# Recurrent layers of a two-block transformer kernel: the gate projection moved behind the head products, the latents behind the query projection, GpSimd made to wait

## What is computed

```python
proj = h @ w_in[l]
c_q, c_kv, k_pe, hq, hf, hi, hg = jnp.split(proj, splits, axis=-1)
a = _mla(c_q, c_kv, k_pe, positions, q_a_norm[l], w_q_b[l], kv_a_norm[l], w_kv_b[l])
r = _hgrn2(hq, hf, hi, hg, lower[l], hg_out_norm[l]).astype(x.dtype)
x = x + jnp.concatenate([a, r], axis=-1) @ w_out[l]
# in _mla: c_q and c_kv are normalized and go through w_q_b and w_kv_b, the rotary parts are
# rotated, then causal scores, softmax, and the product with v
# in _hgrn2: f from hf, q = silu(hq), v = hi, and at the end
o = _rmsnorm(o, out_norm) * jax.nn.silu(g_raw)      # g_raw is hg
```

## Time and profile before

| | us |
|---|---|
| median of 3 runs | 1895.46 |
| lowest, highest | 1894.84, 1895.87 |
| time of the profiled execution | 1896.17 |
| its span in the profile | 1893.6 |
| TensorE busy | 1864.6 |
| VectorE busy | 1530.8 |
| ScalarE busy | 1239.9 |
| GpSimd busy | 404.6 |

### The profile page before, as it was taken

One profiled execution on the slowest core, in us unless ns is written; L12 is line 12 of the kernel. 1 busy time (PEld: TensorE's weight loads), 2 busy tenths in 40 slices (PEclk: granted clock), 3 DMA queues, 4 the chain that ended last, 5 costly groups with the idle time before them and its releaser, 6 DMA issues.

```text
span 1893.6 us, 26114 instructions
## 1 busy us (share of the span) xinstructions
PE 1864.6 (98%) x9344; PEld 1566.7 (83%) x9344; DVE 1530.8 (81%) x1654; ACT 1239.9 (65%) x1484; POOL 404.6 (21%) x206
## 2 busy tenths in 40 slices
PE   9999999999999999999999999999999999999997
PEld 6888889888878888877888888888888888888886
DVE  6745357777776887697699999999999999999997
ACT  6654444444744444464488888888888888888876
POOL 6856870002724000372540000000000000000100
PEclk9999999999999999999999999999999999999999
DMA  9534556665443676444599999999999999999994
GB/s 286 169 120 134 178 182 229 227 219 180 139 139 118 214 239 224 158 125 138 181 386 396 391 383 376 384 397 369 389 365 389 396 363 388 367 389 396 367 396 185
DMA packets 251540, 524.19 MB, mean 277 GB/s; under 512 B 9960, under 2 KB 58736, under 8 KB 251328
## 3 DMA queue, kind: packets, MB, share of 16 engines
q1 hardware_dynamic: 243408, 504.00, 74.4%
q10 hardware_dynamic: 5824, 12.06, 1.7%
q0 software_dynamic: 2224, 7.01, 1.2%
HBM read 507.71 MB, written 15.34 MB: 276 GB/s over the span
## 4 chain that ended last, share of the span: by engine, by line
PE 88%; DVE 6%; ACT 2%; DMA 1%; issue 1%; POOL 1%; SPq 0%; DVEq 0%; ACTq 0%
PE bank L736 24%; PE bank L738 24%; PE bank L737 24%; PE bank L1097 6%; PE bank L1100 3%; DMA arena<-in_w_in 1%; PE bank L1363 1%; PE bank L859 1%; PE bank L832 1%; DVE arena L2440 1%; POOL w_lo_sb L665 1%; DVE arena L1944 1%; DVE arena L2431 1%; PE bank L838 0%; DVE arena L2454 0%
## 5 line engine op out<-in xcount | busy, mean ns | idle before, releaser
L1989 DVE TENSOR_TENSOR w_lo_sb<-arena,w_hi_sb 128x1024 fp32r<-128x1024 f32 x672 | 807.8, 1223 | 73.8 <-ACT w_hi_sb L1517 43.7
L1517 ACT ACTIVATE w_hi_sb<-arena 128x1024 fp32r<-128x1024 f32 x672 | 711.3, 1062 | 168.5 <-PE bank L738 167.8
L736 PE MATMUL bank<-w_hi_sb,left_sb 128*128 128x512 f32 (+1 forms) x1400 | 553.1, 395 | 2.1 <-POOL w_lo_sb L665 2.0
L738 PE MATMUL bank<-w_hi_sb,left_sb 128*128 128x512 f32 (+1 forms) x1400 | 542.2, 387 | 0.0
L737 PE MATMUL bank<-w_lo_sb,left_sb 128*128 128x512 f32 (+1 forms) x1400 | 541.5, 387 | 0.0
L1537 ACT ACTIVATE w_hi_sb<-arena 128x1024 fp32r<-128x1024 f32 (+1 forms) x269 | 278.4, 1052 | 301.4 <-PE bank L738 218.7
L665 POOL TENSOR_TENSOR w_lo_sb<-arena,w_hi_sb 128x1024 fp32r<-128x1024 f32 (+1 forms) x134 | 342.6, 2576 | 546.3 <-ACT w_hi_sb L1537 545.7
L736 PEld LDWEIGHTS bank<-w_hi_sb,left_sb 128*128 128x128 f32 x1400 | 263.1, 188 | 58.8 <-POOL w_lo_sb L665 5.3
L738 PEld LDWEIGHTS bank<-w_hi_sb,left_sb 128*128 128x128 f32 x1400 | 262.9, 188 | 54.8
L737 PEld LDWEIGHTS bank<-w_lo_sb,left_sb 128*128 128x128 f32 x1400 | 263.4, 188 | 50.7 <-issue 0.7
L736 PE MATMUL bank<-w_hi_sb,hid_hi_sb 128*128 128x512 f32 x656 | 257.3, 392 | 0.1
...
...
## 6 DMA issues: line engine op xcount, KB each, us to landing
...
```

The costliest lines, as they stand in the source:

```text
L736: pe.matmul(out, still[0], moving[0], start=start, stop=False)
L738: return pe.matmul(out, still[1], moving[0], start=False, stop=stop)
L1517: act.activation(expert_buffer(w_hi_sb, j), expert_piece(j % MOE_SUBS), ACT.Copy) \
L1989: dve.tensor_tensor(expert_buffer(w_lo_sb, j), expert_piece(j % MOE_SUBS), expert_buffer(w_hi_sb, j).bitcast(F32), ALU.subtract) \
```

## The change

In `gemm_plan` the output gate `hg` moves from behind `hq` to behind the last head product, so that the latents `c0` and `c1` and the values `hi` come three or four pieces earlier. The order on each engine follows. On TensorE the turned decay matrices stand between the pieces of `c0` where they stood between those of `hg`, level 0 follows in `c1`, level 1 and the turned latents in `hi`; the later levels are spread anew, and level 5, the turned rotary parts, both scores, level 6 and level 7 go between the four pieces of `hg`. On ScalarE the pieces of `hg` are made between the exponentials of levels 4, 5 and 6, and the gate is read with a Silu behind the softmax. On VectorE `normalize_c` stands ahead of two levels more; the maxima are taken as minima of negated scores, so that the negations go, for tile 1 in two halves; the gate's multiplication with its gain moves from the middle to the place in front of `gate_hgrn`. GpSimd waits for level 7 ahead of the first piece of `wo`.

```diff
         w = f"w_in_2_{layer}"
         add(f"hf_{layer}", w, base + 512, 512)
         add(f"hq_{layer}", w, base, 512)
-        add(f"hg_{layer}", w, base + 1536, 512)
         add(f"c0_{layer}", w, 0, 512)
         add(f"c1_{layer}", w, 512, base - 512)
...
             add(f"kvb{i}_{layer}", f"w_kv_b_2_{layer}", 512 * i, 512, KV_RANK // P)
+        add(f"hg_{layer}", w, base + 1536, 512)
         add(f"wo_{layer}", f"w_out_2_{layer}", 0, D)
         if layer == 0:
...
-                 (f"hqT_{layer}", 2), *level[0:4], (f"cT_{layer}", 3), *level[4:6], (f"hst_{layer}", 1),
-                 (f"mpT_{layer}", 3), level[6], (f"msc0_{layer}", 2),
-                 level[7], (f"msc1_{layer}", 2), (f"ho_{layer}", 2), (f"mP_{layer}", 3), (f"mo_{layer}", 2),
+                 (f"hqT_{layer}", 2), *level[0:2], (f"cT_{layer}", 3), *level[2:5], (f"hst_{layer}", 1), level[5],
+                 (f"mpT_{layer}", 3), (f"msc0_{layer}", 2), level[6],
+                 (f"msc1_{layer}", 2), level[7], (f"ho_{layer}", 2), (f"mP_{layer}", 3), (f"mo_{layer}", 2),
...
+                        if j == span[f"hg_{l}"][1]:
+                            pool.wait_ge(sem(f"level_ready_{l}"), len(LEVELS))
                     pool.wait_ge(sem("w_hi_ready"), hi_count[j])
                     pool.tensor_tensor(buffer(w_lo_sb, j, k, n), w, buffer(w_hi_sb, j, k, n).bitcast(F32),
...
-                gemm(f"hg_{l}", between={1: turn_gate, 3: turn_queries})
-                gemm(f"c0_{l}", between={0: lambda: level(0), 3: lambda: level(1)})
-                gemm(f"c1_{l}", between={1: lambda: level(2)})
-                gemm(f"hi_{l}", between={0: lambda: level(3), 2: turn_c})
+                gemm(f"c0_{l}", between={1: turn_gate, 3: turn_queries})
+                gemm(f"c1_{l}", between={0: lambda: level(0)})
+                gemm(f"hi_{l}", between={1: lambda: level(1), 3: turn_c})
+                level(2)
                 pe.wait_ge(sem("pair_read"), pair_end[f"cT_{l}"])
...
-                        level(4)
+                        level(3)
                 for i in range(2):
...
+                        level(4)
                 pe.wait_ge(sem("n_kt_ready"), l + 1)
                 b = pair(f"hst_{l}", 0)
...
-                level(6)
-                pe.wait_ge(sem("pair_read"), pair_end[f"mpT_{l}"])
...
-                    if t == 1:
-                        level(7)
+                def turn_rotated():
+                    level(5)
+                    pe.wait_ge(sem(f"m_rot_{l}"), 2 * T)
...
+                def scores(t):
+                    if t == 0:
+                        pe.wait_ge(sem("pair_read"), pair_end[f"mpT_{l}"])
+                        pe.wait_ge(sem("gemm_read"), gemm_at[f"kvb1_{l}"] + T)
...
+                    level(6 + t)
+
+                gemm(f"hg_{l}", between={0: turn_rotated, 1: lambda: scores(0), 2: lambda: scores(1)})
...
-                split_to(span[f"hg_{l}"][0] + 2)
+                split_to(span[f"c0_{l}"][0] + 2)
...
-                split_to(span[f"c0_{l}"][0] + 2)
+                split_to(span[f"c0_{l}"][1] + 2)
...
                 evacuate(f"hq_{l}", by_token(n_q, 0, func=ACT.Silu))
-                evacuate(f"hg_{l}", by_token(n_g, 0, func=ACT.Silu))
...
                 level_exp(2)
-                evacuate(f"c0_{l}", by_token(n_c, 0))
-                level_exp(3)
...
-                level_exp(4)
+                level_exp(3)
                 evacuate(f"hi_{l}", by_token(n_v, 0))
                 evacuate_heads(f"qb0_{l}", n_mqT[:, 0:2, :], n_pq[:, :, 0:128])
-                level_exp(5)
+                level_exp(4)
                 evacuate_heads(f"qb1_{l}", n_mqT[:, 2:4, :], n_pq[:, :, 128:256])
                 evacuate_heads(f"kvb0_{l}", n_mkT[:, 0:2, :], n_vm[:, :, 0:256])
+                split_to(span[f"hg_{l}"][0] + 2)
+                level_exp(5)
+                evacuate_heads(f"kvb1_{l}", n_mkT[:, 2:4, :], n_vm[:, :, 256:512])
+                split_to(span[f"hg_{l}"][1])
                 level_exp(6)
-                evacuate_heads(f"kvb1_{l}", n_mkT[:, 2:4, :], n_vm[:, :, 256:512])
                 level_exp(7)
-                split_to(span[f"kvb1_{l}"][1] + BUFFERS)
-                softmax(n_sc, MLA_HEADS, row_max, f"m_max_ready_{l}", f"m_exp_{l}", keys=(P, TOKENS))
-
+                for t in range(T):
+                    split_to(span[f"hg_{l}"][1] + 1 + 2 * t)
+                    for i in range(MLA_HEADS):
+                        act.wait_ge(sem(f"m_max_ready_{l}"), 1 if t == 0 else 2 + i // 2)
+                        part, at = n_sc[:, t, i, 0:(t + 1) * P], t * MLA_HEADS + i
+                        act.activation(part, part, ACT.Exp, bias=row_max[:, at:at + 1], scale=-1.0,
+                                       accum_out=row_sum[:, at:at + 1]).then_inc(sem(f"m_exp_{l}"), 1)
...
                 level_scale(2)
+                normalize_c()
                 level_take(1)
-                level_diff(4)
-                level_scale(3)
-                level_take(2)
-                normalize_c()
-                rotate(lambda t: n_c[:, t, Q_RANK + KV_RANK:].rearrange("p (h d) -> p h d", h=1), 1)
-                level_take(3)
                 for i in range(3):
                     n = min(2, 5 - 2 * i)
                     b = tiles(bank_of(f"cT_{l}", i)[:, 0:n * TOKENS], n)
                     mul(n_cT[:, 2 * i:2 * i + n, :], b, over(c_gain[l][:, 2 * i:2 * i + n], 2, TOKENS), "pair_read")
+                rotate(lambda t: n_c[:, t, Q_RANK + KV_RANK:].rearrange("p (h d) -> p h d", h=1), 1)
+                level_diff(4)
+                level_scale(3)
+                level_take(2)
+                level_diff(5)
                 level_scale(4)
-                level_diff(5)
-                gains = n_g[:, :, :].rearrange("p t (g d) -> p (t g) d", d=P)
-                mul(gains, gains, over(hg_gain[l], 1, 8))
-                level_take(4)
-                level_scale(5)
+                level_take(3)
                 level_diff(6)
                 dve.wait_ge(sem("gemm_read"), gemm_at[f"qb1_{l}"] + T)
                 rotate(lambda t: n_pq[:, t, :].rearrange("p (h d) -> p h d", h=MLA_HEADS), MLA_HEADS)
+                level_scale(5)
+                level_take(4)
+                level_diff(7)
+                copy_out(f"hst_{l}", 0, n_st)
                 level_scale(6)
                 level_take(5)
-                level_diff(7)
-                copy_out(f"hst_{l}", 0, n_st)
                 for i in range(2):
                     copy_out(f"mpT_{l}", i, n_pqT[:, 2 * i:2 * i + 2, :].rearrange("p k c -> p (k c)"), ROPE)
                 copy_out(f"mpT_{l}", 2, n_pkT, ROPE, TOKENS)
                 level_scale(7)
-                level_take(6)
...
-                    masked_scores(f"msc{t}_{l}", n_sc, MLA_HEADS, (NOPE + ROPE) ** -0.5, causal, [t], (P, TOKENS))
-                    part = row_max[:, t * MLA_HEADS:(t + 1) * MLA_HEADS]
-                    link(dve.tensor_reduce(part, n_sc[:, t, :, 0:(t + 1) * P], AX_X, ALU.max))
...
-                    negate(part, part, f"m_max_ready_{l}")
...
+                    for i in range(2):
+                        heads = slice(2 * i, 2 * i + 2)
+                        b = tiles(bank_of(f"msc{t}_{l}", i)[:, :])
+                        dve.scalar_tensor_tensor(n_sc[:, t, heads, keys], b[:, :, keys], -(NOPE + ROPE) ** -0.5,
+                                                 over(causal[:, t, keys], 1, 2), ALU.mult, ALU.subtract) \
+                            .then_inc(sem("pair_read"), 1)
+                        dve.wait_ge(sem("pair_read"), told("pair_read"))
+                        if (i + 1) * 2 % each == 0:
+                            lo, hi = (i + 1) * 2 - each, (i + 1) * 2
+                            dve.tensor_reduce(row_max[:, t * MLA_HEADS + lo:t * MLA_HEADS + hi], n_sc[:, t, lo:hi, keys],
+                                              AX_X, ALU.min).then_inc(sem(f"m_max_ready_{l}"), 1)
+                    level_take(6 + t)
...
-                split_out(f"mixT_{l}", banks=range(0, 2), freed=span[f"hi_{l}"][1])
+                split_out(f"mixT_{l}", banks=range(0, 2), freed=span[f"hg_{l}"][1])
+                dve.wait_ge(sem("gemm_read"), gemm_at[f"hg_{l}"] + T)
+                gains = n_g[:, :, :].rearrange("p t (g d) -> p (t g) d", d=P)
+                mul(gains, gains, over(hg_gain[l], 1, 8))
                 gate_hgrn()
```

28 lines of the change are left out of this document (13 added, 15 removed).

## The result

| | before | changed |
|---|---|---|
| median of the runs, us | 1895.15 | 1913.41 |
| lowest to highest of four | 1894.23 to 1895.87 | 1910.13 to 1913.85 |
| profiled execution, us | 1896.17 | 1910.13 |
| its span, us | 1893.6 | 1907.8 |
| mean granted clock in it | 0.999 | 0.993 |

The ratio is 1.0092, with an interval of 1.0078 to 1.0107: slower by 18 us. I had forecast slower by 8.6 (1904), with a range to 1908. The direction holds, the size does not.

The account below looks back on a forecast made before the run. TensorE, busy 1864.6 of 1893.6 us, was taken to bound the kernel. Part A -1.6, part B 0 and part C +10.2 gave +8.6 us on 1895.46: 1904.1, rounded to 1904, with a range from 1889 to 1908.

Parts of the forecast that it names:

- Part A: From the first piece of c1 (500.27 in layer 0) to the head products: +0.2 us in layer 0, -1.8 in layer 1.
- part B: From head products to output projection: 4.4 us of old waits filled, 4.4 of new ones made, 0 in each layer.
- part C: Behind the output projection's start: gate products late behind GpSimd's pieces, TensorE waits 5.1 us in each layer.
- the near tie at 4.3: In part C, GpSimd arrives at 4.26, just before VectorE's first reciprocal product ends at 4.30; otherwise the wait is 2.7 us.
- Costs nothing: Extra table load and gate read on ScalarE, SyncE's load queue, and GpSimd's wait for level 7: all hidden, 0 us.
- Rivals 1 to 3: Late gate product costs little, 1894.5 to 1896.3, chance 10; near tie VectorE's way, 1899.3, 12; part B opens, 1895.3, 10.
- Rival 4: Projection pieces fill TensorE's holes and VectorE never waits for GpSimd: -9.8 us, 1885.7, chance 10.
- Rival 5: The clock falls too behind the 5.1 us wait of part C: 4.4 us in all, 1908.5, chance 8.

Follow-up runs that it names:

- e9: The changed kernel with the copy of the state bank ahead of level 7's two subtractions on VectorE: 1914.83 us.
- e10: The changed kernel with level 6's scale on VectorE moved behind the three copies of the turned rotary parts: 1903.22 us.
- e8: The changed kernel without its holding of GpSimd for level 7 before the first piece of the output projection: 1913.27 us.
- e2: The changed kernel with 14 unread matmuls on TensorE before it waits for the gate products: 1910.42 us.
- e1: The changed kernel, GpSimd also waiting before the output projection's fifth piece until VectorE has made both gate products: 1899.42 us.
- e7: The kernel of e1 with 8 unread matmuls on TensorE just ahead of the scores of tile 0: 1894.85 us.
- e5: e1 with state-bank copy, level 5's take and rotary copies ahead of level 7's subtractions and level 6's scale; turned queries given own memory: 1886.95 us.

## Where the prediction was right and where it failed

**The waits were right.** Part A was forecast at +0.2 and -1.8, and came to -0.3 and -2.0. VectorE's chain in part B came out nearly as written: waits of 1.56 and 2.29 for 2.0 and 2.4, the copies at 550.5 against the 29.5 us behind the head products that I had counted (it was 29.2). e9 and e10 show that the two reasons given for them hold, one by one. In part C, VectorE met GpSimd three times, in the order written down, and the products were ready 12.76 us behind the output projection instead of 13.4: 4.5 us a layer for 5.1. The part's own uncertainty, the near tie at 4.3, did go GpSimd's way: its piece began at 4.22, and the second multiplication by the reciprocal waited for it. "Costs nothing" held for the holding at level 7 (e8).

Without the clock, the terms sum to -0.8 (ahead of A), -2.3 (A), +1.3 (B, from 52.33 and 52.30 against 51.68 and 51.64) and +9.0 (C): +7.2, where I had +8.6. That they come so close is in part luck: B came out 1.3 higher, and A, the stretch ahead of it and C 2.7 lower in all. One small sum was off: the work between 550.86 and 574.08 comes to 17.1 us by the figures given with it, not 17.3, so 6.1 us were lost there and not 5.9. No term of the forecast hangs on it.

**The clock was the failing step.** The sum had no term for it. It stood among the rivals, for part C alone, with a chance of 8 and a price of 4.4. What the runs show in its place: behind the waits of part C it costs 3.0 (e2) to 3.7 us (the table), at most 5.0 (all of e1's 14.0 that isn't its waits of 9.0). That is close to the price, but it happens in both layers of every profile that has these waits, so its chance should have been the forecast's. Behind part B's waits it costs 4.6 (e7 against e1), and that was not in the text at all, though I had forecast both waits, 2.0 and 2.4, with one piece of 2.7 us between them. Together that is 7.6 to 9.6 us, about half of the 18.3 that were lost. The experiments price only the one and a half dips that part B of e1 has. The profile of e8, which has all four, gives the whole by the marks of the table: 3.1 and 3.2 us behind part B's waits (55.47 twice, against 52.33 and 52.30) and 2.8 and 1.6 behind part C's (14.61 and 13.38 from `turn_mix` to the next bank, against 11.78 and 11.79), 10.7 in all. With the 7.2 above that is 17.9, and its span is 18.0 longer than that of the kernel before (1911.6 against 1893.6). So nothing else of size is missing from the sum.

I went wrong in how I read the earlier trace rows: the clock fell there some 4.4 us after the last matmul, and I took that for the length of idling that it needs. In the mixers the engine was idle for 1.56 us, worked 3 and was idle for 2.29, and the clock fell at 551 all the same. The Trainium skill, TensorE: Matmul & The Clock Gate, section "What's actually happening", says that the clock depends on how busy the array has lately been. This trace agrees: the pair of waits lowered the clock, and with the second cut to 0.49 (e7) it stayed up. Had I applied that to part B, I might have had a term for it.

**Rivals.** Rivals 1 to 3 are out, by the waits. Rival 4, the pieces fill TensorE's holes and VectorE is never caught (1885.7), is not what this kernel does, but e5 is that case made true, and it took 1886.95. Its condition was right, and its price nearly so. Rival 5 was the right kind and less than half of the size: 4.4 us of clock, with part B missing, where e8's profile has 10.7.
